# A mixture-of-experts layer: gated expert rows accumulated by index into two arrays, in place of rows stored by slot and gathered per token

## The reference, cut to what matters

```python
# each token has two experts and a gate for each; slots are sorted by expert and padded to blocks of 128
xb = x_pad[slot_tok].reshape(nb, MOE_BLOCK, D)
def expert_block(args):
    xblk, e = args
    hid = jax.nn.silu(xblk @ w1[e]) * (xblk @ w3[e])
    return hid @ w2[e]
yb = lax.map(expert_block, (xb, block_expert)).reshape(npad, D)
out = jnp.zeros((T + 1, D), xf.dtype).at[slot_tok].add(yb * slot_gate[:, None].astype(yb.dtype))
# around it:  x2 = x1 + gate_m * out ;  result = RMSNorm(x2) * final_gain
```

## Time and profile before

| | |
|---|---|
| median of 3 runs | 3351.17 us (3344.59 to 3352.19) |
| span of the profiled execution | 3334.9 us; its own whole time is not recorded apart, the median is 16.3 us above the span |
| TensorE busy | 2752.2 us, 83% of the span |
| VectorE, ScalarE, GpSimd busy | 1205.8, 873.4, 630.4 us |
| moved by DMA | 362.02 MB, mean 109 GB/s |
| granted TensorE clock, mean | 0.906 of full |

### The profile page before, as it was taken

One profiled execution on the slowest core, in us unless ns is written; L12 is line 12 of the kernel. 1 busy time (PEld: TensorE's weight loads), 2 busy tenths in 40 slices (PEclk: granted clock), 3 DMA queues, 4 the chain that ended last, 5 costly groups with the idle time before them and its releaser, 6 DMA issues. The chain is left out here.

```text
span 3334.9 us, 39164 instructions
## 1 busy us (share of the span) xinstructions
PE 2752.2 (83%) x12004; PEld 1781.3 (53%) x12005; DVE 1205.8 (36%) x2658; ACT 873.4 (26%) x2061; POOL 630.4 (19%) x769
## 2 busy tenths in 40 slices
PE   6696997969957777776889999996999499999940
PEld 6343443434446676676667777774555344444420
DVE  0233332333334444444445555542222511111138
ACT  0214132141322222222334444442111011111122
POOL 0000000000044444443000000000233110011038
PEclk9997997979978888888699999997999599999975
DMA  6112021120221111111512110006433056889757
GB/s 249 26 45 71 27 71 39 44 71 27 71 76 57 57 57 63 57 57 57 150 65 73 42 42 22 36 18 217 148 117 115 19 189 220 289 306 318 252 217 266
DMA packets 181948, 362.02 MB, mean 109 GB/s; under 512 B 20449, under 2 KB 111585, under 8 KB 180833
## 3 DMA queue, kind: packets, MB, share of 16 engines
q1 hardware_dynamic: 162850, 292.70, 26.0%
q0 software_dynamic: 11648, 41.97, 3.6%
q10 hardware_dynamic: 7360, 26.22, 2.0%
HBM read 252.85 MB, written 108.00 MB: 108 GB/s over the span
## 5 line engine op out<-in xcount | busy, mean ns | idle before, releaser
L613 PE MATMUL pV<-h_transposed,w_in_sb 128*128 128x512 f32 x768 | 339.1, 594 | 0.0
L1956 PE MATMUL hidden_ps<-w,h_rowsT 128*128 x752 | 332.4, 595 | 0.0
L1341 PE MATMUL attn_ps<-values,probs_T 128*128 128x64 f32 x2176 | 297.9, 278 | 40.0 <-DVE probs_T L1304 34.3
L1341 PEld LDWEIGHTS attn_ps<-values,probs_T 128*128 128x128 f32 x2176 | 279.1, 198 | 62.3 <-DVE probs_T L1304 55.8
L1330 PE MATMUL scores<-keys,queries 96*128 96x512 f32 (+3 forms) x640 | 278.3, 568 | 20.7 <-DMA values<-v_d 20.7
L1278 DVE TENSOR_REDUCE block_max<-scores 128x1 f32<-128x512 f32 (+3 forms) x288 | 172.8, 600 | 203.1 <-PE scores L1330 196.9
L1956 PEld LDWEIGHTS hidden_ps<-w,h_rowsT 128*128 128x128 f32 x752 | 143.5, 191 | 181.1 <-issue 181.1
L613 PEld LDWEIGHTS pV<-h_transposed,w_in_sb 128*128 128x128 f32 x768 | 145.2, 192 | 172.9 <-issue 169.7
L1570 PE MATMUL out_ps<-w_out_sb,yT 128*128 128x512 f32 x512 | 226.6, 601 | 2.2 <-DVE yT L1535 2.2
L1229 ACT ACTIVATE probs<-scores,neg_max 128x512 f32<-128x512 f32 (+3 forms) x320 | 197.3, 626 | 46.3 <-DVE neg_max L1289 45.1
L1071 PE MATMUL bankW<-Y_g,U 128*128 128x128 f32 x640 | 144.3, 312 | 47.6 <-ACT Y_g L881 47.1
(11 more groups left out here) (329 smaller groups left out, 3985.3 us busy)
## 6 DMA issues: line engine op xcount, KB each, us to landing
w<-in_w_dram SPq DMA_DIRECT2D x64, 1024.0 KB, 10.3
w_sb<-in_w_dram SPq DMA_DIRECT2D x32, 1024.0 KB, 13.2
ys_d<-expert_y ACTq DMA_DIRECT2D x46, 512.0 KB, 7.2
w_mod_rows<-in_w_mod_dram SPq DMA_DIRECT2D x8, 2048.0 KB, 7.2
ys_d<-zero_rows SPq DMA_DIRECT2D x16, 1024.0 KB, 5.9
kqv<-qkv_d SPq DMA_DIRECT2D x16, 768.0 KB, 4.2
x_in<-in_x_dram SPq DMA_DIRECT2D x18, 512.0 KB, 4.0
mod_w<-in_w_mod_dram SPq DMA_DIRECT2D x2, 4096.0 KB, 21.7
```

The lines of the kernel that those rows point to most:

```text
L613: last = pe.matmul(pV[n % 2][:], win[:, k, QKV0 + n * P:QKV0 + (n + 1) * P], hT[:, k, :], start=(k == 0), stop=(k == ND - 1))
L1341: last = pe.matmul(pO[i % 2][:, h], probT[:, gi % RING, t], v[:, kt, h * DV:(h + 1) * DV], start=(kt == 0), stop=(kt == i))
L1956: last = pe.matmul(pH[par][:], xT[par][:, k], m.w13[:, ds(slot, 1), k].rearrange("p s n -> p (s n)"), start=(k == 0), stop=(k == ND - 1))
```

## The change

Rows are no longer stored by slot. VectorE multiplies both halves of `expert_ps` by the slot's gate and by `gate_m` on the way to `expert_y`, and GpSimd adds the 128 rows to HBM by index with an accumulating DMA: blocks with `par` 0 onto `x1_d`, those with `par` 1 onto a second array `y2_d` that `attention` has filled with zeros. Two blocks in flight thus never touch one array, and a block waits until the accumulate two before it has landed. Padding slots go to 128 spare rows behind the 2048. `routing` computes for each slot also the gate and the row. `finish` takes the place of `combine`: it loads a tile of both arrays, five ahead, adds them, and normalises.

```diff
# attention, SP
-                sp.dma_start(m.ys_d[(nsure + i * per) * P:(nsure + (i + 1) * per) * P, :].rearrange("(b p) n -> p b n", p=P),
-                             zeros[:].unsqueeze(1).to_broadcast([P, per, D])).then_inc(zeros_stored, 16)
+                sp.dma_start(m.y2_d[i * P:(i + 1) * P, :], zeros[:]).then_inc(zeros_stored, 16)
...
             sp.dma_start(m.y_d[(NT - 1) * P:, 0:AH * DV], y[:]).then_inc(y_stored, 16)
+            sp.dma_start(m.y2_d[T:, :], zeros[:]).then_inc(zeros_stored, 16)
# routing
-                last = pe.matmul(pS[:], rowhot[n // NT][:, n % NT], blkhot[n // NT][:, n % NT], start=(n == 0), stop=(n == 2 * NT - 1))
+                last = pe.matmul(pS[:].rearrange("p a b -> p (a b)"), rowhot[n // NT][:, n % NT],
+                                 blkhot[n // NT][:, n % NT].rearrange("p a b -> p (a b)"), start=(n == 0), stop=(n == 2 * NT - 1))
...
-                ins = dve.tensor_tensor(blkhot[k][:], blkhot[k][:], over(tok[:], NB), ALU.mult)
+                do(dve.tensor_tensor(blkhot[k][:, :, 0], blkhot[k][:, :, 1], over(tok[:], NB), ALU.mult))
+                ins = dve.tensor_tensor(blkhot[k][:, :, 1], blkhot[k][:, :, 1], over(gates[:, k], NB), ALU.mult)
...
-            do(dve.tensor_copy(m.slot_token[:, 0:NB], pS[:]))
+            do(dve.tensor_copy(slot_v[:], pS[:, 0]))
+            do(dve.tensor_copy(m.slot_gate[:, 0:NB], pS[:, 1]))
+            do(dve.tensor_scalar(m.slot_token[:, 0:NB], slot_v[:], 1.0, 0.0, ALU.subtract, ALU.max))
+
+            do(dve.tensor_scalar(empty[:], slot_v[:], 0.0, spare[:, 0:1], ALU.is_equal, ALU.mult))
+            do(dve.scalar_tensor_tensor(out=m.slot_row[:, 0:NB], in0=slot_v[:], scalar=-1.0, in1=empty[:], op0=ALU.add, op1=ALU.add))
# experts, GpSimd
+            def add(b, par):
+                wait(y_added[par], (b - par) * 8 - START)
+                pool.tensor_copy(row[par][:], m.slot_row[:, ds(b, 1)]).then_inc(row_copied, 1)
+                wait(row_copied, b + 1)
+                wait(y_ready, b * 2 + 2)
+                pool.indirect_dma_start((m.x1_d, m.y2_d)[par], bass.IndirectOffsetOnAxis(ap=row[par][:, 0:1], axis=0), y[:, par], None,
+                                        compute_op=ALU.add).then_inc(y_added[par], 16)
...
-            with pool.Fori(0, n) as i:
-                gather(i * 2 + 2, 0)
-                gather(i * 2 + 3, 1)
...
+            with pool.Fori(1, n) as i:
+                gather(i * 2 + 4, 0)
+                add(i * 2, 0)
+                gather(i * 2 + 5, 1)
+                add(i * 2 + 1, 1)
# experts, ScalarE
-                act.copy(y[:, par, 0:512], pY[:, 0]).then_inc(y_act, 1)
...
-                act.dma_start(m.ys_d[ds(b * P, P), :], y[:, par]).then_inc(y_stored[par], 16)
# experts, VectorE
-                dve.tensor_copy(y[:, par, 512:], pY[:, 1]).then_inc(y_dve, 1)
+                wait(row_copied, b + 1)
+                for half in range(2):
+                    at = slice(half * 512, (half + 1) * 512)
+                    dve.scalar_tensor_tensor(out=y[:, par, at], in0=pY[:, half], scalar=m.slot_gate[:, ds(b, 1)],
+                                             in1=m.gate_m[:, at], op0=ALU.mult, op1=ALU.mult).then_inc(y_ready, 1)
# experts, TensorE
-                wait(y_act, b)
-                wait(y_dve, b)
+                wait(y_ready, b * 2)
# combine becomes finish: SP, GpSimd, VectorE
+                sp.dma_start(xa[:, t], m.x1_d[t * P:(t + 1) * P, :]).then_inc(x_loaded[t], 16)
+                sp.dma_start(xb[:, t], m.y2_d[t * P:(t + 1) * P, :]).then_inc(x_loaded[t], 16)
...
-                pool.tensor_tensor(x2[:, b], s1[:], xr[:, t % DEPTH], ALU.add).then_inc(x2_ready, 1)
-                if t + DEPTH < NT:
-                    gather(t + DEPTH)
...
-                dve.scalar_tensor_tensor(out=s1[:], in0=yb[:, t % DEPTH], scalar=m.gates[:, 1, t:t + 1], in1=s0[:, t % 2],
-                                         op0=ALU.mult, op1=ALU.add).then_inc(sum_step, 1)
-                dve.wait_ge(sum_step, 2 * t + 1)
-                dve.tensor_tensor(s1[:], s1[:], m.gate_m, ALU.mult).then_inc(sum_step, 1)
+                dve.tensor_tensor(x2[:, t % 4], xa[:, t % DEPTH], xb[:, t % DEPTH], ALU.add).then_inc(x2_ready, 1)
```

More of the change, by code:

```diff
@@ L1169, in _ @@
             load_kv(sp, 2)
-            nsure = 2 * T // P
-            per = (NB - nsure) // NT
-            assert per * NT == NB - nsure
-            sp.wait_ge(mask_made, 3)
+            sp.wait_ge(zeros_made, 1)
             for i in range(NT):
@@ L1641, in routing @@
         rowhot = [sb(f"row_hot{k}", [P, NT, P]) for k in range(2)]
-        blkhot = [sb(f"blk_hot{k}", [P, NT, NB]) for k in range(2)]
+        blkhot = [sb(f"blk_hot{k}", [P, NT, 2, NB]) for k in range(2)]
+        slot_v, empty, spare_i, spare = sb("slot_value", [P, NB]), sb("slot_empty", [P, NB]), sb("spare_i", [P, 1], I32), sb("spare_row", [P, 1])
         ebf = sb("block_expert_f", [1, NBT])
-        pR, pC, pS = ps("rank_ps", [P, NT * NE]), ps("total_ps", [P, NT * NE]), ps("slot_ps", [P, NB])
+        pR, pC, pS = ps("rank_ps", [P, NT * NE]), ps("total_ps", [P, NT * NE]), ps("slot_ps", [P, 2, NB])
         const, chain, exps, counted, slotted = (sem(n) for n in ("route_const", "chain", "route_exp", "counted", "slotted"))
@@ L1696, in first_of @@
                 do(dve.tensor_tensor(dst, dst, tmp[:, :, 0:k], ALU.mult))
-            dve.wait_ge(const, 5)
+            dve.wait_ge(const, 6)
+            do(dve.tensor_copy(spare[:], spare_i[:]))
             do(dve.tensor_copy(iota_f[:], iota_i[:]))
             do(dve.tensor_copy(tok[:], tok_i[:]))
+            do(dve.tensor_scalar(tok[:], tok[:], 1.0, None, ALU.add))
             g = lg[:, :, 0:NG]
@@ L1791, in experts @@
         idx = [sb(f"row_index{i}", [P, 1], I32) for i in range(2)]
+        row = [sb(f"out_row{i}", [P, 1], I32) for i in range(2)]
         hg = [sb(f"h_rows{i}", [P, D]) for i in range(2)]
@@ L1804, in experts @@
         hT_ready, hT_copied, down_ready = sem("hT_ready6"), sem("hT_copied6"), sem("down_ready")
-        y_act, y_dve = sem("y_act6"), sem("y_dve6")
-        y_stored = [sem(f"y_stored6_{i}") for i in range(2)]
+        y_ready, row_copied = sem("y_ready6"), sem("row_copied")
+        y_added = [nc.alloc_semaphore(f"y_added{i}") for i in range(2)]
         def pairs(eng):
@@ L1860, in _ @@
             gather(1, 1)
-            with pool.Fori(0, n) as i:
-                gather(i * 2 + 2, 0)
-                gather(i * 2 + 3, 1)
-            wait(gathered[0], n * 16 + 16 - START)
-            wait(gathered[1], n * 16 + 16 - START)
+            gather(2, 0)
+            gather(3, 1)
+            gather(4, 0)
+            add(0, 0)
+            gather(5, 1)
+            add(1, 1)
+            with pool.Fori(1, n) as i:
[3 more added lines that the diff above has]
+                add(i * 2 + 1, 1)
+            for par in range(2):
+                wait(y_added[par], n * 16 - START)
+            wait(gathered[0], n * 16 + 32 - START)
+            wait(gathered[1], n * 16 + 32 - START)
         @block.scalar
@@ L1901, in _ @@
                 body(i * 2 + 1, 1)
-            for p in range(2):
-                held_wait(act, y_stored[p], n * 16, wait_point)
         @block.vector
@@ L1988, in _, with finish @@
                 body(i * 2 + 1, 1)
-def combine(nc, m, final_norm, out):
+def finish(nc, m, final_norm, out):
     with nc.cleanup_on_exit(), ExitStack() as ctx:
@@ L2013, in _ @@
             for t in range(NT):
                 sp.wait_ge(out_ready, t + 1)
-                sp.dma_start(out[0, t * P:(t + 1) * P, :], ob[:, t % 2]).then_inc(stored[t % 2], 16)
+                sp.dma_start(out[0, t * P:(t + 1) * P, :], ob[:, t % 4]).then_inc(stored[t % 4], 16)
                 if t + DEPTH < NT:
-                    sp.dma_start(xr[:, t % DEPTH], m.x1_d[(t + DEPTH) * P:(t + DEPTH + 1) * P, :]).then_inc(x_loaded[t % DEPTH], 16)
-            for i in range(2):
-                sp.wait_ge(stored[i], 16 * NT // 2)
+                    sp.dma_start(xa[:, t % DEPTH], m.x1_d[(t + DEPTH) * P:(t + DEPTH + 1) * P, :]).then_inc(x_loaded[t % DEPTH], 16)
+                    sp.dma_start(xb[:, t % DEPTH], m.y2_d[(t + DEPTH) * P:(t + DEPTH + 1) * P, :]).then_inc(x_loaded[t % DEPTH], 16)
@@ L2021, in _ @@
+            for i in range(4):
+                sp.wait_ge(stored[i], 16 * NT // 4)
         @block.gpsimd
         def _(pool):
[L2023 to L2038 removed]
+            for t in range(NT):
@@ L2079, in _ @@
                 dve.wait_ge(powed, 2 * t + 2)
-                if t >= 2:
-                    dve.wait_ge(stored[t % 2], 16 * (t // 2))
-                dve.scalar_tensor_tensor(out=ob[:, t % 2], in0=x2[:, t % 2], scalar=rs[:, t % 2:t % 2 + 1], in1=fgain[:],
+                if t >= 4:
+                    dve.wait_ge(stored[t % 4], 16 * (t // 4))
+                dve.scalar_tensor_tensor(out=ob[:, t % 4], in0=x2[:, t % 4], scalar=rs[:, t:t + 1], in1=fgain[:],
```

(2 more changed lines are left out.)

96 lines of the change are left out of this document (35 added, 61 removed).

## The result

| | before | after |
|---|---|---|
| median | 3347.88 us (4 runs, 3344.31 to 3352.19) | 3300.44 us (4 runs, 3297.08 to 3303.20) |
| ratio | | 0.9877 (95%: 0.9853 to 0.9902) |
| span of the profiled execution | 3334.9 us | 3295.3 us |
| the same again, in a later session | 3338.70 us (7 runs) | 3298.68 us (4 runs), ratio 0.9884 (0.9867 to 0.9900) |

The change gains 1.2%: 47 us by the medians of the first comparison, 40 by those of the second, 39.6 between the two profiled spans.

The account below looks back on a forecast made before the run. TensorE bounds the expert blocks (DMA near its edge), GpSimd `combine`. Terms -44.4 (`finish`), +4 (experts' end), +5.5 (`routing`), +1 (`attention`), +10 (weight stall) sum to -23.9: 3351.2 to 3327 us, range 3310 to 3375.

Parts of the forecast that it names:

- The base: Whole kernel: starts from the 3351.17 us median, carrying over unchanged 16.3 us outside the 3334.9 us profiled span.
- The rate of `finish`: Last stage: DMA binds, 25.7 MB at 365 GB/s plus an 8.4 us tail, 121.4 to 77 us: -44.4.
- The stall for the weights: Expert loop: accumulates at 2.7 us of all DMA engines delay weight loads, so TensorE waits: +10 us (0 to +42).
- with no margin: Saturated single-block experts, 44.6 us to 3002.8: 3.9 accumulates add 5.7 us, and TensorE stands 5.7 us.
- 345 GB/s for all of it: Expert loop: DMA rate assumed in the account over all 28 loads, giving 12 us lost at 2.73 us per `y`.
- `routing`: Routing stage: extra VectorE passes and operations, and slot matmuls of 128 columns for 64: +5.5 us (+3.5 to +10.5).
- The end of `experts`: After the last block: second VectorE pass, accumulate issue and landing, barrier before the last stage: +4 us (+1 to +8).
- What I had at nothing in the loop: Expert loop: GpSimd's new waits and VectorE's second pass cost nothing if an accumulate lands within 22 us.
- `attention`: Attention's end: the last zero-row store, 0.52 MB, stands behind the last store of `y`: +1 us.
- A: Expert loop: accumulate costs little more than a store (1.26 to 2.0 us), TensorE never waits; -34, 3317; chance 0.24.
- C: Expert loop: weights become the bound in dense stretches, 42 to 67 us lost, 3359 to 3384; chance 0.16.
- D: Expert loop: accumulates set the pace, 15.9 us per block for 11.39, whole time 3524; chance 0.11.

Follow-up runs that it names:

- run 7: Changed kernel, but `finish` loads only the first of the two arrays and adds it to itself (output not the layer's): 3289.25 us, ratio 0.9844.
- run 1: Changed kernel, but `y_ready` counts blocks instead of halves, so TensorE needs no extra register instruction before the down-projection: 3295.26 us, ratio 0.9883.
- run 2: Changed kernel, but the indirect DMA overwrites the rows instead of adding to them (output not the layer's): 3301.09 us, ratio 0.9894.
- run 3: Changed kernel, but every accumulate is issued a second time, into two arrays that nothing reads: 3342.86 us, ratio 1.0011.
- Run 5: Kernel before, but the slot matmuls in `routing` carry 128 columns instead of 64, the second 64 unused: 3336.60 us, ratio 0.9981.
- run 8: Changed kernel, but GpSimd issues the accumulate of block b ahead of the gather of block b+4: 3300.46 us, ratio 0.9888.
- run 10: Changed kernel, `y_ready` counting blocks, SP loading eight `finish` tiles before the barrier, gain loaded at `experts` start, spare zero rows stored early: 3290.35 us, ratio 0.9853.
- run 9: Changed kernel, `y_ready` counting blocks, SP loading five `finish` tiles, then the gain, at the end of `experts` after the last accumulates: 3297.00 us, ratio 0.9867.

## Why the prediction was wrong

The direction was right, and so were the bounds of both stages and the price of an accumulate. The time came out 27 us below the forecast of 3327, by two faults: the gain is 39.6 us by the spans where I had 23.9, and the base was too high by 11.

**The base.** "16.3 us lie outside the span and I carry them over unchanged" is the step that put the time below the range. In every run whose span is on record, of any kernel, the time is 1.7 to 1.8 us above it. The 16.3 were mostly that the three timed runs of the kernel before were slower than the profiled one, and nothing carried that over: the median of the changed kernel is 5.1 us above its profiled span. With the true gain, 3351.2 - 39.6 = 3311.6 would still have lain in the range.

**The size.** The difference of 15.6 has these parts.

- **The rate of `finish`** (-44.4 forecast, -53.5). "A mix with stores I put at 365". It ran at 411 over 3232 to 3288. The bytes, the tail (8.4 forecast, 8.2 from the last `x` to the end) and the bound were right; run 7 shows the bound. I took a value between 306, which was GpSimd's pace and no limit of DMA, and 390, which I called loads only, though GpSimd's gathers ran beside them. At 411 the forecast's own sum gives 60.1 + 1.5 + 8.4 = 70, so that 7 of the 9 are the rate; the rest no run separates: **9 us**.
- **The stall for the weights** (+10, measured 0.1, and 0.5 in run 1). The accumulate's price was right, 2.8 us for 2.7, and q0's share 36.4% for 36%. The Trainium skill ("Collectives: The Full Stack", the section on the fold count) would have made it 1.93 copies, a ratio measured on a ring of four ranks; here it is 2.8 / 1.26 = 2.2, and 2.1 against the indirect write of run 2, so the measured ratio is a little higher than the page's. What failed is "with no margin". These are the 45 us of the saturated run, before and after:

```profile
2958.00:3003.00 45.00, 45.00 (x136) 22.04 (x134) 7.22 (x12) 7.27 (x16) 4.62 (x8) 1.00 0.90 319
```

```profile
2960.00:3005.00 45.00, 45.00 (x136) 22.02 (x134) 9.83 (x16) 4.93 (x12) 12.06 (x16) 1.00 1.02 322
```

  The DMA share was 0.90, and the 5.7 us that I added for this stretch found room: it rose by 0.12, which is 5.4 us. The account carried on over the loop had the same fault in "345 GB/s for all of it", fitted to one landing as if the engines alone had set its time, while the earlier trace rows had 379 in the same run. Run again, the account gives 0.2 us at 385 GB/s and 3.0 at 375 with one accumulate, 28 and 35 with two; at 345, 12 and 67. Measured were 0.1 and 33. That is an estimate by a model which no run tests apart; run 2 shows that nothing of the price reaches the time, and run 3 that twice the price does: **9.9 us**.
- **`routing`** (+5.5, measured -0.9, and -1.4 behind it). VectorE's extra passes came as counted. The slot matmuls were costed by scaling columns at the clock of before; at that clock the columns cost nothing, and with 128 of them TensorE came to full clock, so that VectorE waited 3.2 us for 8.2. Run 5 shows the effect by itself, -3.9. Of the -1.4 behind it, 1.3 are the first 32 matmuls of the up-projection, 14.65 us for 15.95; run 5 has only 0.3 of it. The same code took 53.9 to 55.1 us, and 24.9 to 25.6 behind it, in the ten profiles of the changed kernel and its variants, so up to 1.8 us of this are of the one profile: **7.8 us**.
- **The end of `experts`** (+4, measured +10.3). Landing was 6.0 us for 6.1. Missing was GpSimd's drain. Before, the last indirect transfer of the stage was a gather issued at 3183.5, whose drain of 4.0 us was over before TensorE was done; the change puts an accumulate at the very end: **-6.3 us**.
- **What I had at nothing in the loop** (measured +4.2). The new waits block nothing, as argued, and run 8 shows the slack. But one costs an instruction on TensorE (run 1): **-4.2 us**.
- **`attention`** (+1; the next stage follows the last store 1.4 us later, and run 10 takes it back). The whole stretch up to `routing` is 1.7 longer: **-0.7 us**.

9 + 9.9 + 7.8 - 6.3 - 4.2 - 0.7 leave 15.5. The three largest errors went the same way: each time I took the dearer side of what the rows allowed.

Of the rivals, A came nearest in time, though not for its reason: the accumulate did cost both a read and a write, and was hidden. C and D, with 0.27 of the chance, were all on the slower side, and no rival made `finish` or `routing` cheaper than the forecast. Run 3 shows C's mechanism at work with twice the accumulates.

## What to carry to other kernels

Before carrying the difference between a timed median and a profiled span over to another kernel, ask what it is made of: here all but 2 us of it belonged to single executions. Take the capacity of the DMA engines from stretches where their share is near 1 and no engine sets the pace, and read their share over the very stretch to which a cost is added; "no margin" was 0.90 here, and the stall did not come. When a software DMA moves to the end of a stage, count from its issue to the end of GpSimd's drain, and look for loads that need not wait for the barrier (6.9 us here, once the load that is waited for first was also issued first and eight tiles were loaded ahead). On the engine that sets the pace, look at the program order for new register instructions: 0.09 us times 45 was a tenth of this change's gain.

## What the runs showed of the hardware

- An accumulating indirect DMA of 128 rows of 4 KB takes 1.60 us to issue, 2.8 us of all 16 engines and 8.8 us at the median to land; the overwriting one takes 0.99 us to issue and 1.3 us of the engines.
- GpSimd's DRAIN ended 10.0 to 12.0 us behind the last indirect issue in the changed kernel and its variants, whether GpSimd waited for the landing before it or not, but 9.0 us behind it in run 3, and 8.2 us behind the last gather in the kernel before.
- The 64 matmul records of one group took 0.42 us each, one every 0.21, with 64 and with 128 columns at 1.2 GHz; with 128 columns the granted clock rose to 2.4 GHz after 15 to 26 of them, and the rest took 0.275, one every 0.11.
- Plain loads and stores mixed ran at 411 to 419 GB/s on one core, and plain loads alone at 415 (run 9); the 390 of the earlier trace rows had GpSimd's gathers beside the loads.
- A single-column power on GpSimd takes 0.55 us, and 1.41 beside a wide pass of VectorE.
